# First projection in halves of its contraction, and four modulation units summed by VectorE

## The reference, cut to what matters

```python
silu_c = silu(c)                                     # 1024 numbers
shift, scale, gate = split(silu_c @ ada_w[0] + ada_b[0], 3)
h = rmsnorm(x) * norm_g[0] * (1 + scale) + shift     # 256 x 1024
z = h @ even_in_w[0]                                 # 1024 -> 5120 columns
```

## Time and profile before

| | us |
|---|---|
| median of 3 runs | 929.41 (929.21 to 931.08) |
| the profiled execution, its own time | 931.61 |
| span of that execution | 929.8 |
| PE busy in the span | 909.5 (98%) |
| DVE busy | 653.2 (70%) |
| ACT busy | 511.5 (55%) |
| TensorE clock granted, mean | 0.998 |

### The profile page before, as it was taken

One profiled execution on the slowest core, in us unless ns is written; L12 is line 12 of the kernel. 1 busy time (PEld: TensorE's weight loads), 2 busy tenths in 40 slices (PEclk: granted clock), 3 DMA queues, 4 the chain that ended last, 5 costly groups with the idle time before them and its releaser, 6 DMA issues.

```text
span 929.8 us, 19585 instructions
## 1 busy us (share of the span) xinstructions
PE 909.5 (98%) x8673; PEld 886.9 (95%) x8673; DVE 653.2 (70%) x771; ACT 511.5 (55%) x611; POOL 2.1 (0%) x14
## 2 busy tenths in 40 slices
PE   8899999999999999999999999999999999999997
PEld 7899999998999999999998999899899999999997
DVE  3887988775677667767789886557777665465565
ACT  3445444444644567954485764376656553455445
POOL 0000000000000000000000000000000000000000
PEclk9999999999999999999999999999999999999999
DMA  9999547775577544467634453334444556556421
GB/s 337 367 366 360 187 137 243 261 230 170 163 230 247 182 136 137 136 199 231 196 109 142 137 172 98 92 91 144 141 159 137 182 191 222 178 186 219 162 92 46
DMA packets 153439, 172.30 MB, mean 185 GB/s; under 512 B 4000, under 2 KB 137692, under 8 KB 153228
## 3 DMA queue, kind: packets, MB, share of 16 engines
q1 hardware_dynamic: 151696, 167.43, 55.5%
q10 hardware_dynamic: 1660, 3.63, 1.2%
HBM read 170.00 MB, written 1.05 MB: 184 GB/s over the span
## 4 chain that ended last, share of the span: by engine, by line
PE 80%; DVE 8%; ACT 6%; DMA 3%; issue 3%; DVEq 0%; POOL 0%; ACTq 0%; POOLq 0%
PE pj L2755 65%; DVE w_lo L1538 2%; ACT w_hi L1026 2%; DMA raw<-in_ada_w_dram 1%; DVE cst_phase L1512 1%; DMA work<-in_x_dram 1%; PE pj L2709 1%; DMA raw<-in_even_out_w_dram 1%; PE pj L2711 1%; PE pj L2710 1%; PE pj L2683 1%; DMA raw<-in_odd_in_w_dram 1%; PE m_all L2445 1%; PE m_all L2428 1%; DVE work L1983 1%
## 5 line engine op out<-in xcount | busy, mean ns | idle before, releaser
L1538 DVE TENSOR_TENSOR w_lo<-raw,w_hi 128x2048 fp32r<-128x2048 f32 (+1 forms) x126 | 285.5, 2268 | 130.5 <-ACT w_hi L1026 130.1
L2755 PE MATMUL pj<-h_hi,w_hi 128*128 128x256 f32 x1160 | 328.7, 283 | 0.4 <-issue 0.4
L2755 PE MATMUL pj<-h_lo,w_hi 128*128 128x256 f32 x1160 | 323.8, 279 | 0.0
L2755 PE MATMUL pj<-h_hi,w_lo 128*128 128x256 f32 x1160 | 323.6, 279 | 0.0
L1026 ACT ACTIVATE w_hi<-raw 128x2048 fp32r<-128x2048 f32 (+1 forms) x126 | 238.0, 1890 | 49.5 <-PE pj L2755 23.1
L2755 PEld LDWEIGHTS pj<-h_hi,w_hi 128*128 128x128 f32 x1160 | 217.3, 187 | 3.5 <-issue 2.2
L2755 PEld LDWEIGHTS pj<-h_lo,w_hi 128*128 128x128 f32 x1160 | 217.4, 187 | 0.4
L2755 PEld LDWEIGHTS pj<-h_hi,w_lo 128*128 128x128 f32 x1160 | 217.3, 187 | 0.2
L2755 PE MATMUL pj<-y_lo,w_hi 128*128 128x256 f32 x624 | 174.2, 279 | 0.0
L2755 PE MATMUL pj<-y_hi,w_hi 128*128 128x256 f32 x592 | 165.6, 280 | 0.0
L2755 PE MATMUL pj<-y_hi,w_lo 128*128 128x256 f32 x592 | 165.1, 279 | 0.0
(11 more groups left out here) (426 smaller groups left out, 1147.6 us busy)
## 6 DMA issues: line engine op xcount, KB each, us to landing
raw<-in_odd_in_w_dram SPq DMA_DIRECT2D x28, 1024.0 KB, 5.3
raw<-in_w_in_dram SPq DMA_DIRECT2D x23, 1024.0 KB, 5.3
raw<-in_ada_w_dram SPq DMA_DIRECT2D x22, 1024.0 KB, 7.8
raw<-in_w_ff_in_dram SPq DMA_DIRECT2D x16, 1024.0 KB, 5.4
raw<-in_w_ff_out_dram SPq DMA_DIRECT2D x16, 1024.0 KB, 5.1
raw<-in_even_in_w_dram SPq DMA_DIRECT2D x13, 1024.0 KB, 5.1
raw<-in_even_out_w_dram SPq DMA_DIRECT2D x8, 1024.0 KB, 5.2
raw<-in_odd_out_w_dram SPq DMA_DIRECT2D x8, 1024.0 KB, 5.3
```

The lines of the kernel that those rows point to most:

```text
L1538: V.tensor_tensor(lo[:, 0:n], raw_of(u)[:, 0:n], hi[:, 0:n].bitcast(F32), ALU.subtract).then_inc(done, 1)
L2755: m = nc.tensor.matmul(to, a_, b_, start=(s == 0 and q == 0 and (fb == 0 or not together)), stop=(s == len(steps_) - 1 and q == 2), skip_g ...
```

## The change

1. The four ev units of 8 row blocks become eight of 4 row blocks (512 KB). Loads in order: x (now second on SP's queue), n = 0 to 3, ev0 to ev2 first halves, n = 4 to 7, ev3 first half, four second halves, then n = 8, 9, 10, ea0, n = 11, ea1. `SPL` is still 3: at each part ACT and DVE split up to the half that stands two places behind it in the list of projection units, and DVE sums the modulation units that lie between them in the list on the way. PE multiplies ev0 to ev2 by blocks 0 to 3 of `h`, then does n = 5 and 7, ev3's first half, and the four second halves.
2. `ADA_PE` shrinks to (0, 2): DVE sums n = 4 to 7 (4 and 5, 6 and 7 into one sum each), and PE adds up partitions for the pairs. n = 8, 9, 10 stay behind ev.
3. The small vectors are loaded and turned in two parts: 7 by POOL at the start (`params` 0), 15 by ACT after ev (`row_loads`, `params` 1).
4. DVE modulates blocks 1 and 3 of the first half, ACT 0 and 2; the scaling of x is cut in two (`first_scale`). Fewer idle matmuls at the start, three more (`BUSY["first"]`) ahead of ev.
5. In `gla_z` two small copies that only carried semaphores are gone.

```diff
-EARLY = {3: 8, 4: 16, 5: 24, 9: 116, 11: 124, 15: 116, 17: 124, 19: 116, 21: 124}
-REUSED = {9: 3, 11: 4, 15: 9, 17: 11, 19: 15, 21: 17}
+EARLY = {3: 8, 4: 16, 5: 20, 9: 100, 10: 108, 11: 28, 15: 24, 19: 116, 21: 124, 23: 116, 25: 124}
+REUSED = {9: 3, 10: 4, 11: 5, 15: 9, 19: 10, 21: 11, 23: 19, 25: 21}
-BUSY = {"norm1": (8, 2), "ffn": (1, 2), "gate": (1, 2)}
+BUSY = {"first": (3, 3), "norm1": (8, 2), "ffn": (1, 2), "gate": (1, 2)}
-ADA_PE = (0, 2, 4, 6)
+ADA_PE = (0, 2)
...
+    a0, a1, a2, a3 = ada_units((0, 0, 0, 0), (0, 0, 0, 1), (0, 1, 0, 0), (0, 1, 0, 1))
+    ev_first = ev_units(0, range(3))
+    second_ada = ada_units((0, 0, 1, 0), (0, 0, 1, 1), (0, 1, 1, 0), (0, 1, 1, 1))
+    ev_first += ev_units(0, (3,))
+    ev_second = ev_units(1, range(4))
+    behind_ev = ada_units(*[later_ada.pop(0) for _ in range(3)])
...
     step("load_x")
+    schedule.append(a0)
     step("first_sum")
+    step("params", 0)
+    schedule.append(a2)
+    step("first_scale", 0)
+    schedule.extend((a1, a3))
     step("first_split")
     step("ada_half", 0)
+    step("keep_busy", "first")
     step("modulate", 0)
+    step("first_scale", 1)
+    for i in range(3):
+        ev_part(i, 0)
+    schedule.extend(second_ada)
     step("ada_half", 1)
     step("modulate", 1)
+    ev_part(3, 0)
+    for i in range(4):
+        ev_part(i, 1)
+        if i:
+            schedule.append(behind_ev[i - 1])
     step("sgu_w")
+    step("row_loads")
     even("ea", "copy", even_w, 0)
...
+        part_end = {(("ev", i), half): units[u]["slot"] + SPL for half, us in enumerate((ev_first, ev_second)) for i, u in enumerate(us)}
...
+                elif kind == "part":
+                    if split_to is None:
+                        job_part(*what)
+                    else:
+                        split_to(part_end[what])
+                        if what[1]:
+                            job_part(what[0])
...
             sp.dma_start(c_rows, ins["c"].rearrange("a (n p) -> (a n) p", p=P)).then_inc(S("c_in"), 16)
+            sp.dma_start(ar(0, 8).rearrange("p (n c) t -> p n (c t)", n=2), x_in).then_inc(S("x_in"), 16)
...
+            load_rows(pool, 0, ROWS_A, "rows_a_loaded", N_ROWS_A_LOADS)
...
-                for _ in range(5):
+                for _ in range(3):
                     nc.tensor.matmul(M[1][:, 0:T], K("ones"), cst[:, 0:T], start=True, stop=True)
...
-                for _ in range(4):
-                    nc.tensor.matmul(PJ[1][:, 0:T], K("ones"), cst[:, 0:T], start=True, stop=True)
+                nc.tensor.matmul(PJ[1][:, 0:T], K("ones"), cst[:, 0:T], start=True, stop=True)
```

More of the change, by code:

```diff
@@ L210, in even, with ada_units, ev_units, ev_part @@
         for i in range(4):
-            job(name, kind, i, layout_, [ev0_unit if (name, i) == ("ev", 0) else unit(w, 0, KD, c0 + i * CB, CB)], KD, 0, HR(0))
+            job(name, kind, i, layout_, [unit(w, 0, KD, c0 + i * CB, CB)], KD, 0, HR(0))
             if i in ADA_BEHIND[name]:
                 ada(*later_ada.pop(0))
+    def ada_units(*which):
+        made = []
+        for w in which:
+            ada(*w)
+            made.append(schedule.pop())
+        return made
+    def ev_units(half, cols):
+        return [unit(even_w, 4 * half, 4, 2048 + i * CB, CB) for i in cols]
+    a0, a1, a2, a3 = ada_units((0, 0, 0, 0), (0, 0, 0, 1), (0, 1, 0, 0), (0, 1, 0, 1))
[5 more added lines that the diff above has]
+    for i in range(4):
+        job("ev", "copy_t", i, "T", [ev_first[i], ev_second[i]], 4, 0, HR(0))
+        schedule.pop()
+    def ev_part(i, half):
+        schedule.append(("part", (("ev", i), half)))
     step("load_x")
-    ada(0, 0, 0, 0)
-    ada(0, 0, 0, 1)
+    schedule.append(a0)
     step("first_sum")
[L219 to L222, removed]
+    step("params", 0)
+    schedule.append(a2)
+    step("first_scale", 0)
+    schedule.extend((a1, a3))
     step("first_split")
-    step("params")
     step("ada_half", 0)
-    ada(0, 0, 1, 0)
-    ada(0, 0, 1, 1)
+    step("keep_busy", "first")
     step("modulate", 0)
-    ada(0, 1, 1, 0)
-    ada(0, 1, 1, 1)
-    step("second_split")
+    step("first_scale", 1)
+    for i in range(3):
+        ev_part(i, 0)
+    schedule.extend(second_ada)
     step("ada_half", 1)
     step("modulate", 1)
-    even("ev", "copy_t", even_w, 2048, "T")
+    ev_part(3, 0)
+    for i in range(4):
+        ev_part(i, 1)
+        if i:
+            schedule.append(behind_ev[i - 1])
     step("sgu_w")
+    step("row_loads")
     even("ea", "copy", even_w, 0)
     step("sgu_v")
+    step("params", 1)
     for i in range(4):
@@ L564, in program @@
     visits = 0
-    for j in jobs.values():
+    for u in ev_first + ev_second:
+        visits += 1
+        units[u]["visited"] = visits
+    for i in range(4):
+        jobs["ev", i]["projected"] = 5 + i
+    for key, j in jobs.items():
+        if key[0] == "ev":
+            continue
         for u in sorted({u for u, _, _ in j["steps"]}):
@@ L1557, in first_sum, with params @@
                 V.tensor_tensor(flat(E_["sq"], 4), flat(E_["sq"], 4), flat(E_["sq"] + 4, 4), ALU.add).then_inc(S("x_scaled"), 1)
+            def params(half):
+                if half == 1:
+                    dve.wait_ge(S("params"), 2)
+                    link(V.tensor_scalar(one_less_mu, vec("rwkv_mu_2", 0, 14), -1.0, 1.0, ALU.mult, ALU.add))
             def ada_half(half):
@@ L2685, in ada_unit @@
                     else:
-                        m = nc.tensor.matmul(pair_sums(n // 2)[:, cols_], acc_of(n)[:, cols_], K("ones"), start=False, stop=(fb == 3), skip_group_check=True)
+                        m = nc.tensor.matmul(pair_sums(n // 2)[:, cols_], acc_of(n)[:, cols_], K("ones"), start=(n >= 4 and fb == 0), stop=(fb == 3), skip_group_check=True)
                 m.then_inc(S("ada_used"), 1)
@@ L2734, in run_job @@
                     order_.sort(key=lambda sf: (sf[1], sf[0]))
+                if half is not None:
+                    order_ = [(s, fb) for s, fb in order_ if s // 4 == half]
                 for at, (s, fb) in enumerate(order_):
```

178 lines of the change are left out of this document (87 added, 91 removed).

## The result

| | before | after |
|---|---|---|
| median, us | 929.41 (5 runs, 929.14 to 931.08) | 934.45 (5 runs, 933.62 to 937.09) |
| profiled execution: own time / span | 931.61 / 929.8 | 934.11 / 932.0 |
| mean granted clock of it | 0.998 | 0.994 |

Ratio 1.0048, interval 1.0033 to 1.0064: 5.0 us slower, where 2.0 were forecast and the range ended at 933.4.

A forecast was written before the change was run, and what follows sets the result against it. The weight stream bounds the opening, PE and the stream nearly together the stretch behind it. +1.8 us at ea0 and +0.2 at ea2 sum to +2.0 us on the median 929.41: 931.4, range 928.8 to 933.4.

The forecast's parts named there:

- The sign and the main mechanism: Slower: in the opening VectorE's sums become the longest chain, SP's queue runs dry at n=8 and n=9, ea0 +1.8 us.
- The step that failed first: PE's wait from 34 to 42 us may halve the clock, but ev3's first half has 2.8 us to hide in.
- Rival C: PE idles some 3 us before ea0 and TensorE's clock falls: 1.7 us more, +3.7, 933.1; chance 0.15.
- A: The forecast: the stream runs dry at n=8 and n=9, ea0 late by 1.8 us; 931.4, chance 0.5.
- The second: Behind ea0: ea1 +1.8 us, ea2 +1.8 to +2.3, from ea3 on the delay neither larger nor given back.
- ea1's load "in time": At ea1: load in at 65.3, split at 69.5, PE free at 69.9, start +1.8 us.
- 0 to 0.5 us for ea2: At ea2: load at 71.0, ready between 75.3 and 76.1, PE free at 75.6; +0.2 us taken as the middle.
- from ea3 on: Behind ea2: loads have 3 us of slack or more, PE has no gap, the delay stays unchanged.
- the forecast's own term, 1.8: At ea0: load lands at 59.5, 3.9 us late, ea0 ready at 63.7 against 61.91: +1.8 us.
- D: Faster: ev's first half moves ahead, DVE is not late, ea0 ready at 59.8: -2.1 us, 927.3; chance 0.13.

The follow-up runs named there:

- experiment 1: Changed kernel with idle matmuls in PE's two long waits, ahead of n=7's and n=9's ones: 935.55, ratio 1.0052.
- experiments 2 and 3: Changed kernel with n=8's load in its own place: 934.89, ratio 1.0048; the same plus idle matmuls in both PE waits: 934.01, ratio 1.0032.
- Experiment 9: Changed kernel with idle matmuls before n=7's ones, n=8's own place, n=9's ones behind ev3's second half, ea0 ahead of n=10: 929.80, ratio 1.0005.
- experiment 10: Experiment 9 without the idle matmuls ahead of n=7's ones: 932.62, ratio 1.0033.
- experiments 9 and 11: Experiment 9 (929.80, ratio 1.0005), and that kernel with ea1, ea2 and ea3 each one modulation unit ahead too: 930.06, ratio 0.9998.
- the control: Kernel before (whole units, PE multiplying n=4 and 6) with ea0 to ea3 one modulation unit ahead of their places: 928.45, ratio 0.9976.
- experiment 5: Kernel before with VectorE summing n=4 and n=6 too, whole units and old places kept: 936.48, ratio 1.0064.
- experiment 4: Changed kernel with PE multiplying n=4 and n=6 again as before, halves and load order kept: 934.73, ratio 1.0046.

## Why the prediction was wrong

**What held.** The sign and the main mechanism: the sums make VectorE the longest chain of the opening (40.85 for 40.7, 43.12 for 43.0, ev1's second half 47.32 + 1.22 = 48.5 for 48.4), n = 8 waits for ev0's split and the queue runs dry (window 42 to 44: 50 GB/s), n = 9's load is issued at 48.57 for 48.4, ea0's load lands at 59.77 for 59.5. With the clock held up, experiment 1 has ea0 at 64.00 for the forecast 63.7. (The 17.8 MB "ahead of ea0" count ea0's own unit as well, on both sides, which changes nothing.)

**The step that failed first** is the sentence that the earlier wait of PE "may also halve the clock, but ev3's first half then has the 2.8 us" to hide in. The wait was seen, the fall was priced at nothing, and the cover was not there. 2.8 us is what ev3's first half takes at the full clock, so nothing is left to hide in: with the clock up (experiment 1) it ends at 45.03, just as block 4 of `h` is complete (VectorE's part at 44.9), and with the fall it ends at 47.40. ev0's second half stands behind it, ACT's copy of ev0 and its rounding of ev3's last half behind that, and then VectorE's split and sums. The term should have been 2.3 us on VectorE (ev3's last split at 52.01 against 49.69 in experiment 1), 2.0 of them idle. Rival C had the right mechanism, in front of ea0. The second fall came in front of ev3's second half, because n = 9's ones stand there, a place that the prediction did not look up although it had named n = 9 as late. The rule of the Trainium skill that stood beside C ("TensorE: Matmul & The Clock Gate", section "HAM oscillation — how this bites in real kernels": waits for the next weights between bursts put the array back on its half clock) agrees with this trace for the waits of 4.82 and 3.19 us, with 1.16 against 2.07 us for the same eight matmuls, though here PE waited for VectorE's sums and not for weights. The measured 934.45 lies nearer to C's 933.1, which had a chance of 0.15, than to A's 931.4.

**The second** is that the delay of ea0 stays what it is: ea1's load "in time", 0 to 0.5 us for ea2, and "from ea3 on ... PE runs on without a gap, so the delay is neither made larger nor given back". Experiment 1 shows its size without any fall: a lag of 2.3 at ea0's end becomes 3.1 by ea2 and 3.7 by 151 us. The forecast put ea1's and ea2's loads at 65.3 and 71.0, each a fixed distance behind ea0's; they landed at 66.31 and 72.13. ea2's is not spaced by the stream: it waits for its place until ea0 is split (63.97). The same in experiments 2 and 3: issue at 64.38 and 61.97, on the end of ea0's split each time. Why ea1's load came 6.7 us behind ea0's instead of 5.77 was not followed up. Experiment 9 leaves the chain as it is (issue at 58.96, ea0's split done at 58.89) but starts it 5 us earlier, and together with the idle matmuls and n = 8's place that takes the loss away.

**How the 5.0 us divide.** Without any fall ea0 starts 2.3 us late (64.00 against 61.66): the forecast's own term, 1.8, and 0.5 because before's ea0 started 0.25 ahead of the forecast's 61.91 and the new one 0.3 behind 63.7. The falls bring ea0 another 1.1 (64.00 to 65.09). That makes 3.4; 0.3 more stands at the norm (after 4.4 at 207 us, of which before's longer wait there gives 0.7 back), 0.3 lies outside the span. The last 1.0 is in no single place of the two traces: before lost 1.6 us at the norm in its profiled execution and the changed kernel did not, and the medians lie 2.2 under and 0.3 over their profiled executions. The mean clock of before's 78 runs beside the experiments went from 0.993 to 1.000, that of the changed kernel's five from 0.989 to 0.994. The shares are not independent: without the falls (experiment 1) the loads take the gain. But the falls do count once the loads are ahead: experiment 10 without the idle matmuls is 0.28% slower than experiment 9 with them. Parts 3 to 5 of the change (small vectors, scaling of x, copies) were not taken out by themselves; in experiments 9 and 11 they are all in, and the time is before's. Why the time outside the span is 2.1 us in all kernels with both halves and VectorE's sums, and 1.8 in all others, stays open.

**D** was ruled out rightly, but for a reason that was too narrow: it asked only whether the halves get ahead, and when they did (experiments 9 and 11, ea0 2.7 to 2.9 us early) the time was before's. With all the repairs they end level with before, and the control without halves and sums is 0.2% faster.

## What to carry over

When work moves from an engine that waits to one that does not, follow the new longest chain into the ring: a place that is released late turns a late split into a late load one round on, and that lasts. Price each idle stretch of PE of 3 us or more with a fall of the clock, give one for the shorter ones a chance, and follow what stands right behind it on PE, not only what looks critical. Before splitting work into finer parts, try the order of the loads: here that alone, four units moved one place ahead, gave a better time than the halves with every repair, though how it does so is not shown.

## What the runs showed of the hardware

Every idle stretch of PE of more than 3 us had the half clock behind it: 3.19, 3.49, 3.52, 4.55, 4.82 and 7.44 us (the 5.24 of experiment 5 lies in the same low stretch as the 7.44). Shorter ones went both ways. At the norm the granted clock was 0.58 over 4 us behind 2.19 us (before) and behind only 1.16 us (experiment 4, 216 to 220), and it was 1.00 behind the changed kernel's 1.49. Earlier in the kernel it was 1.00 behind 1.62 us (experiment 9), 2.56 us (before, until 26.1) and 2.91 us (the control, until 26.6). So the length of one wait does not settle it below 3 us:

```profile
216.00:220.00 4.00, 4.00 (x13) 3.21 (x12) 2.10 (x6) 2.20 (x6) 0.00 (x0) 0.58 0.67 221
```

```profile
22.00:28.00 6.00, 3.09 (x28) 2.90 (x27) 4.58 (x3) 3.07 (x4) 0.00 (x0) 1.00 1.06 383
```

The first is experiment 4 behind its 1.16 us, the second the control around its 2.91. A fall took 1.7 to 2.4 us where it was read (ev3's second half 4.5 for 2.8, ea0's first half 5.3 for 2.9). In all five runs with them, nine calls of idle matmuls in the wait of 4.82 left 0.93 or 0.94 us idle and the clock at 1.00. A load that goes into the place of a unit two rounds back was issued within 0.1 us of the end of that unit's split and landed 7.0 to 8.1 us later (ea2's, in the changed kernel and experiments 1, 2, 3 and 9).

A repair of one limit can be invisible until the next is repaired too: ratios 1.0052 and 1.0048 for one each, 1.0032 for both, 1.0005 with the order of ea0's load.
